# A streaming encoder step: token halves carried through the whole second layer, with S5, gated unit, norms and outputs of one half placed in the feed-forward passes of the other

## The chip, the cores and the metric

The kernel runs as one program on 1 core of a Trainium2 chip. The metric is the device time of one execution in microseconds. Five engines run their own instruction streams and meet at semaphores: PE (matrix products), DVE (vector work), ACT (activations, casts and some DMA issues), POOL (further vector work and some DMA issues) and SP (which issues most DMAs).

## What is computed

1088 tokens (1024 of a prompt, 64 of a running stream) of width 1024 go through two layers. Cut to what matters here:

```python
def swiglu(h, w_gate, w_up, w_down):            # w_gate, w_up: 1024 x 2816
    return (jax.nn.silu(h @ w_gate) * (h @ w_up)) @ w_down

def s5_mixer(h, ...):                           # 64 groups of 16 channels, 64 complex states each
    x = einsum('gpc,blgc->blgp', bb, ug)        # complex, into the states
    s = associative_scan(s_t = a * s_(t-1) + x_t)
    y = real part of einsum('gcp,blgp->blgc', c, s) + d_skip * u
    gl = gelu(y) @ w_glu                        # 1024 x 2048
    ga, gb = split(gl, 2)
    return ga * sigmoid(gb), s_last

# layer 0: x += attention heads and spatial gating, joined by one output projection; x += swiglu(rmsnorm(x))
# layer 1: x += s5_mixer(rmsnorm(x)); x += swiglu(rmsnorm(x))
# y = rmsnorm(x); also the new keys, values, gating rows and the last S5 states
```

## The kernel before

Activations lie transposed: 1024 features are 8 tiles of 128 partitions, tokens run along the free axis. A dense product is made of three single-pass products (`three`, L251 to L253): high part of the weights by high part of the input, the same by the low part, low part of the weights by the high part. Weights come in slabs of 512 KB: SP loads one (L234, two buffers `raw`), ACT makes the high part `whi` (L241), POOL subtracts and leaves `wlo` (L245); SP may load slab t only when POOL has made `wlo` of slab t - 2, and a slab's buffers come free when PE has left the slab four (in layer 1 six) before. A slot of the middle stage is the work on one slab, or on half of one.

The stages in time: input projection; a middle stage whose order a planner writes as a list of slots; S5; GLU; norm 3; feed-forward of layer 1; output.

The middle stage (`SLOTS`, `mid_sp`, `mid_act`, `mid_pool`, `mid_dve`, `mid_pe`) holds attention, output projections and layer 0's feed-forward. It works on two token halves: A has 512 tokens, B 576 in chunks of 288 + 288 (`HCH`). Half A's feed-forward pass runs beside the last attention steps, then comes B's output projection (`outB`, 8 slots of one slab), then half B's pass. A pass has 66 slots: gate, up, gate, up, and two of down, 11 times. Each engine walks the list and does its share of every slot (so does SP: the slab for two slabs on, then what else the slot names). Three banks of PSUM take the results in turn; ACT takes up gates, DVE ups (product) and downs (sum into x). The other half's squares, norm sums and scaled tiles lie in slots of the pass that runs. `mst` (L1211) is the gathered mixer output, and L1315 makes its low part lB for `outB`.

S5 (`s5_sp`, `s5_pe`, `s5_act`, `s5_pool`, `s5_dve`) then takes all 1088 tokens, 8 time steps folded into the partitions, so that 136 columns are left, in 8 units of 8 groups. In each unit PE transposes B (L1829), multiplies C by powers into a kernel K (L1837), makes x (L1849) and y (L1867 with the shift matrix `tm`, L1869 with the states `sh`); K goes through DVE (`kt`) and eight DMAs of SP (L1802) into `tm`; u, C and E come by DMA (L1787, L1776); DVE runs the scan (L1949 to L1983: products L1931, scans L1964 and L1965). y goes out to memory in eight DMAs and comes back reordered. GLU, norm 3 and the feed-forward of layer 1 work on all tokens in chunks of 384/384/320; GLU's inputs hlo are made by L2018, its result is added to x by L2064, and L349 adds squares. The output transposes 9 tiles of 128 (the last 64) tokens (L2081).

## Time and profile before

| | us |
|---|---|
| median of 3 runs | 2808.97 (2808.0 to 2819.7) |
| the profiled execution | 2815.95 |
| its span in the trace | 2814.2 |
| PE matmul busy | 2569.8 (91%) |
| PE weight load busy | 2368.4 (84%) |
| DVE, ACT, POOL busy | 1165.5 (41%), 879.8 (31%), 1108.1 (39%) |
| mean granted clock of PE | 0.938 of full speed |

The slices of the page show where an engine was busy over the span, in tenths; each is 70 us. Busy time of PE counts matmuls whose ends are modelled. A row of the timeline gives start and duration, and in brackets the idle time before with what released it. "Records" of a plain fp32 product are two to an instruction.

### The profile page before, as it was taken

Reading aid. Unit: us, or ns where it says so; the run is one execution under the profiler, and the core shown is the slowest. Engines: PE = TensorE matmul, PEld = TensorE weight load, DVE = VectorE, ACT = ScalarE, POOL = GpSimd, SP = SyncE. Lnnn points to the kernel's source line nnn. Section 1 sums busy time; section 2 is a strip of 40 time slices with the busy share of each in tenths; the row PEclk is TensorE's granted clock in tenths of the full one; section 3 lists DMA queues with packets and bytes.
Section 4 is the critical chain, followed back from the end, with each engine's and each line's share of the span. In section 5 each row is a group of like instructions: output and inputs, shape, how many; then the busy total and the mean of one; then the engine's idle time right before and its main releaser. Section 6 shows DMA issues by size and latency. Waiting matters only on the chain.

```text
span 2814.2 us, 38283 instructions
## 1 busy us (share of the span) xinstructions
PE 2569.8 (91%) x15274; PEld 2368.4 (84%) x15274; DVE 1165.5 (41%) x1877; ACT 879.8 (31%) x1304; POOL 1108.1 (39%) x770
## 2 busy tenths in 40 slices
PE   6998948989997999999999588799699999999998
PEld 4898936667776978999999466799599999999997
DVE  3696636665562142422222677322412222222224
ACT  3422236688893332212211221311311111111114
POOL 2555534554464565544444200333532222222223
PEclk9999969989998999999999676899899999999999
DMA  4315665313423223322222575311111111111111
GB/s 121 103 59 202 240 185 130 86 51 101 104 72 130 85 75 98 107 89 78 86 83 70 162 203 148 125 46 46 30 42 42 44 41 42 44 45 45 45 45 64
DMA packets 290435, 254.10 MB, mean 90 GB/s; under 512 B 32560, under 2 KB 254704, under 8 KB 289024
## 3 DMA queue, kind: packets, MB, share of 16 engines
q1 hardware_dynamic: 264624, 201.73, 24.5%
q0 software_dynamic: 7088, 31.15, 2.9%
q10 hardware_dynamic: 18592, 19.40, 2.9%
q8 instruction: 91, 1.49, 0.2%
q14 instruction: 40, 0.33, 0.0%
HBM read 195.08 MB, written 54.80 MB: 89 GB/s over the span
## 4 chain that ended last, share of the span: by engine, by line
PE 74%; DVE 10%; DMA 5%; POOL 4%; ACT 3%; issue 2%; SPq 1%; ACTq 1%; POOLq 0%; DVEq 0%
PE ps L251 22%; PE ps L253 22%; PE ps L252 22%; PE ps L983 2%; DVE v L1931 1%; PE ps L995 1%; PE ps L1869 1%; DMA mst<-mT 1%; DVE fbuf L423 1%; POOL hlo L431 1%; PE ps L1867 1%; DVE t L1706 1%; POOL ssum L349 1%; DMA dC<-co 1%; PE ps L975 1%
## 5 line engine op out<-in xcount | busy, mean ns | idle before, releaser
L245 POOL TENSOR_TENSOR wlo<-raw,whi 128x1024 fp32r<-128x1024 f32 x250 | 606.1, 2434 | 428.1 <-ACT whi L241 426.4
L251 PE MATMUL ps<-hhi,whi 128*128 128x384 f32 (+1 forms) x1920 | 636.7, 332 | 49.0 <-POOL hlo L2018 14.8
L252 PE MATMUL ps<-hlo,whi 128*128 128x384 f32 (+1 forms) x1920 | 632.3, 329 | 0.0
L253 PE MATMUL ps<-hhi,wlo 128*128 128x384 f32 (+1 forms) x1920 | 632.2, 329 | 0.0
L251 PEld LDWEIGHTS ps<-hhi,whi 128*128 128x128 f32 x1920 | 365.9, 191 | 54.7 <-issue 22.2
L252 PEld LDWEIGHTS ps<-hlo,whi 128*128 128x128 f32 x1920 | 365.9, 191 | 0.3 <-issue 0.2
L253 PEld LDWEIGHTS ps<-hhi,wlo 128*128 128x128 f32 x1920 | 365.6, 190 | 0.0
L241 ACT ACTIVATE whi<-raw 128x1024 fp32r<-128x1024 f32 x250 | 259.1, 1053 | 319.2 <-PE ps L253 141.1
L251 PE MATMUL ps<-hB,whi 128*128 128x288 f32 x832 | 247.4, 297 | 12.2 <-POOL lB L1315 12.2
L509 POOL TENSOR_TENSOR gl<-fbuf,gh 128x384 f32 (+3 forms) x66 | 63.8, 967 | 490.3 <-DVE gh L564 490.3
L253 PE MATMUL ps<-hB,wlo 128*128 128x288 f32 x832 | 246.6, 296 | 0.0
L252 PE MATMUL ps<-lB,whi 128*128 128x288 f32 x832 | 246.5, 296 | 0.0
L561 DVE TENSOR_TENSOR fbuf<-ps,abuf 128x384 f32<-128x384 f32 (+1 forms) x66 | 35.3, 535 | 453.5 <-ACT abuf L479 449.2
L479 ACT ACTIVATE abuf<-ps 128x384 f32<-128x384 f32 (+1 forms) x66 | 31.2, 474 | 561.5 <-PE ps L253 561.5
L251 PE MATMUL ps<-rh,whi 128*128 128x288 f32 (+1 forms) x528 | 177.6, 336 | 15.4 <-DVE xA L1363 6.4
L572 DVE TENSOR_TENSOR x<-ps,x 128x384 f32<-128x384 f32 (+1 forms) x264 | 141.2, 535 | 110.0 <-PE ps L253 108.8
L1353 DVE TENSOR_TENSOR fb<-ps,ab 128x288 f32<-128x288 f32 (+1 forms) x66 | 35.3, 535 | 363.4 <-PE ps L253 339.8
L252 PE MATMUL ps<-rl,whi 128*128 128x288 f32 (+1 forms) x528 | 175.3, 332 | 0.0
L253 PE MATMUL ps<-rh,wlo 128*128 128x288 f32 (+1 forms) x528 | 175.1, 332 | 0.0
L253 PE MATMUL ps<-gh,wlo 128*128 (+2 forms) x528 | 172.2, 326 | 0.0
L251 PE MATMUL ps<-gh,whi 128*128 (+2 forms) x528 | 172.1, 326 | 0.0
L252 PE MATMUL ps<-gl,whi 128*128 (+2 forms) x528 | 172.1, 326 | 0.0
(315 smaller groups left out, 4803.6 us busy)
## 6 DMA issues: line engine op xcount, KB each, us to landing
raw<-in_ffn_w_gate SPq DMA_DIRECT2D x66, 512.0 KB, 3.9
raw<-in_ffn_w_up SPq DMA_DIRECT2D x66, 512.0 KB, 3.9
raw<-in_ffn_w_down SPq DMA_DIRECT2D x66, 512.0 KB, 3.6
raw<-in_ab_w_in SPq DMA_DIRECT2D x20, 512.0 KB, 4.2
raw<-in_ab_w_out SPq DMA_DIRECT2D x16, 512.0 KB, 3.7
raw<-in_ssm_w_glu SPq DMA_DIRECT2D x16, 512.0 KB, 3.9
dC<-co POOLq DMA_DIRECT2D x4, 1152.0 KB, 4.5
ca<-dC SPq DMA_DIRECT2D x8, 576.0 KB, 4.9
```

Of the source, the lines that this page charges most:

```text
L241: act.activation(whi[:, slot(t), :], raw[:, t % 2, :], ACT.Copy).then_inc(sem("w_hi"), 1)
L245: pool.tensor_tensor(wlo[:, slot(t), :], raw[:, t % 2, :], whi[:, slot(t), :].bitcast(F32), ALU.subtract).then_inc(sem("w_lo"), 1)
L251: pe.matmul(out, wh, rh, start=first, stop=False)
L252: pe.matmul(out, wh, rl, start=False, stop=False)
L253: return pe.matmul(out, wl, rh, start=False, stop=last)
L349: pool.tensor_tensor(ssum[:, c, 0:n], ssum[:, c, 0:n], sqbuf(k, a)[:, 0:n], ALU.add).then_inc(sem("n_add"), 1)
L479: act.activation(abuf[:, v % 2, 0:n], ps[:, 2 * (v % 2), 0:n], ACT.Silu).then_inc(sem("pair_act"), 1)
L509: pool.tensor_tensor(gl[:, bass.ds(o, n)], fbuf[:, v % 2, 0:n], gh[:, bass.ds(o, n)].bitcast(F32), ALU.subtract).then_inc(sem("hid_lo"), 1)
L561: dve.tensor_tensor(fbuf[:, v % 2, 0:n], ps[:, 2 * (v % 2) + 1, 0:n], abuf[:, v % 2, 0:n], ALU.mult).then_inc(sem("pair_used"), 1)
L572: dve.tensor_tensor(xo, acc(v)[:, 0:n], xo, ALU.add).then_inc(sem("acc_used"), 1)
L983: mm = pe.matmul(out, mat[:], r, start=mat is tri and u["first"] and j == 0, stop=True, skip_group_check=True)
L1353: dve.tensor_tensor(fb2[:, h % 2, 0:n], out, ab2[:, h % 2, 0:n], ALU.mult).then_inc(sem("use_v"), 1)
```

## The change

The last serial stages are dissolved into the slot list. There are four passes of 66 slots now: layer 0 half A, layer 0 half B, layer 1 half A, layer 1 half B. All work of layer 1 that isn't a pass is put into slots of the pass that runs:

- S5 of half A (64 columns) stands in the pass of layer 0, half B; S5 of half B (72 columns, starting from the scan state that half A leaves) in the pass of layer 1, half A. A unit begins in a gate slot with x (PE, ACT's copy, DVE's scan), y follows two slots later, the next unit's loads three, the return of y four and six slots later; one unit every six slots.
- GLU of half A stands in 16 slots before the last three stages of the pass of layer 0, half B; GLU of half B likewise in the pass of layer 1, half A. Norm 3 of a half has its 8 tiles per chunk in the slots behind: for A four a slot, for B eight a slot.
- Output tiles of half A stand in the pass of layer 1, half B; those of half B at the end.
- The tables of S5 (B transposed, and the shift matrix of K) are made once for both halves, in 8 steps two slots apart in and around the slots of `outB`, and kept in memory (`dBT`, `dT`); both halves load them (`s5_load`).
- Chunks of half B are 256 + 320. All 332 slabs use four buffers. Activation tables are preloaded by ACT only in steps after another table was used. The tokens x stay in SBUF between the layers.

The diff cut to its core:

```diff
 HALF = [(0, 512), (512, 576)]
-HCH = [[(0, 512)], [(512, 288), (800, 288)]]
+HCH = [[(0, 512)], [(512, 256), (768, 320)]]
...
+        passes = [(0, 0), (0, 1), (1, 0), (1, 1)]
+
+        def sequence():
+            for no, (layer, half) in enumerate(passes):
+                if no != 1:
+                    yield "pair", layer, half, 0
+                for i in range(PARTS):
+                    yield "pair", layer, half, 2 * i + 1
+                    if i + 1 < PARTS:
+                        yield "pair", layer, half, 2 * i + 2
+                    elif no == 0:
+                        yield ("pair", *passes[1], 0)
+                    yield "down", layer, half, i
...
+                soon(5, pl=[0])
+                for f in range(KD):
+                    soon(7 + 2 * f, pre=[f])
+                    if f + 1 < KD:
+                        soon(8 + 2 * f, pl=[f + 1])
+                    soon(8 + 2 * f, psh=[f])
+                    soon(9 + 2 * f, pst=[f])
...
+            for k, h, at in list(stage["rms"]):
+                if now >= at:
+                    stage["rms"].remove((k, h, at))
+                    rms_slot(k, h)
+                    end = norm_soon(k, h, 1, 8 if (k, h) == (3, 1) else 4)
+                    if k == 2:
+                        soon(end, hs=[h])
+                        soon(end + 1, sl=[8 * h])
+                        stage["f"][h], stage["free"][h] = 0, len(SLOTS) + end + 3
+
+        def run_glu(h):
+            stage["glu"][h] = -1
+            glu(h)
+            rms_slot(3, h)
+            norm_soon(3, h, 1, 4 * (h + 1))
...
+                for h in range(2):
+                    f = stage["f"][h]
+                    if gate and f is not None and f < KD and len(SLOTS) >= stage["free"][h]:
+                        F = 8 * h + f
+                        work["sx"] = [F]
+                        stage["f"][h], stage["free"][h] = f + 1, len(SLOTS) + 5
...
+                for F in work.get("sx", []):
+                    soon(2, sy=[F])
+                    if F % KD < KD - 1:
+                        soon(3, sl=[F + 1])
+                    soon(4, sz=[F])
+                    soon(6, sg=[F])
+                    if F % KD == KD - 1:
+                        for i in range(4):
+                            soon(7 + i, ys=[KD * (F // KD) + 2 * i, KD * (F // KD) + 2 * i + 1])
+                        stage["glu"][F // KD] = len(SLOTS) + 8
...
+                for f in S["psh"]:
+                    pre_shift(sp, f)
+                for f in S["pst"]:
+                    pre_store(sp, f)
+                for f in S["pl"]:
+                    pre_load(sp, f)
+                for h in S["hs"]:
+                    h_store(sp, h)
+                for F in S["sl"]:
+                    s5_load(sp, F)
...
+        def pre_load(sp, f):
+            if f == 0:
+                sp.wait_ge(sem("u_pv"), NU)
+                sp.wait_ge(sem("ms_lo"), 12)
+            else:
+                sp.wait_ge(sem("s_K"), f)
+            js = slice(4 * f, 4 * f + 4)
+            sp.dma_start(br[:], dB[:, js, :, :]).then_inc(sem("br_in"), 16)
+            sp.dma_start(cp[:], dC[:, js, :, :]).then_inc(sem("cp_in"), 16)
...
+        def pre_pe(pe, f):
+
+            pe.wait_ge(sem("br_in"), 16 * (f + 1))
+            if f:
+                pe.wait_ge(sem("e_BT"), 2 * f)
+                pe.wait_ge(sem("e_K"), 2 * f)
+            else:
+                pe.wait_ge(sem("u_c"), NU)
+                pe.wait_ge(sem("u_t"), NU)
+            for q in range(8):
+                mm = pe.transpose(ps[:, 3 + q // 4, (q % 4) * P:(q % 4 + 1) * P], br[:, q // 2, q % 2, :], ident[:])
+            mm.then_inc(sem("s_B"), 1)
+            pe.wait_ge(sem("cp_in"), 16 * (f + 1))
+            for g in range(8):
+                j, a = divmod(g, 2)
+                r = slice(64 * a, 64 * a + 64)
+                for q in range(2):
+                    mm = pe.matmul(ps[0:16, 5 + a, j * P:(j + 1) * P], br[r, j, q, P - 16:P], cp[r, j, q, 0:P],
+                                   start=q == 0, stop=q == 1)
+            mm.then_inc(sem("s_K"), 1)
...
+        def pre_shift(sp, f):
+
+            sp.wait_ge(sem("e_BT"), 2 * f + 2)
+            sp.dma_start(dBT[:, 4 * f:4 * f + 4, :, :], btp[:]).then_inc(sem("bt_out"), 16)
+            sp.wait_ge(sem("e_K"), 2 * f + 2)
+            if f:
+                sp.wait_ge(sem("t_out"), 16 * f)
+            else:
+                sp.wait_ge(sem("t_zero"), 1)
+            for s in range(L):
+                sp.dma_start(tmp[16 * s:16 * s + 16, :, 16 * s:P], kt[0:16, :, 0:P - 16 * s]).then_inc(sem("t_made"), 16)
...
+        def s5_x_pe(pe, F):
+            h, f = divmod(F, KD)
+            nn = NN[h]
+            pe.wait_ge(sem("bt_in"), 16 * (F + 1))
+            pe.wait_ge(sem(f"u_in{F % 2}"), 16 * L * (F // 2 + 1))
+            if F:
+                pe.wait_ge(sem("e_X"), banks_of(F - 1))
+            else:
+                pe.wait_ge(sem("e_BT"), 2 * KD)
+            for q in range(2):
+                for j in range(4):
+                    o = (4 * q + j) * nn if h == 0 else j * nn
+                    for a in range(2):
+                        mm = pe.matmul(ps[64 * a:64 * a + 64, 3 + (q if h else 0), o:o + nn],
+                                       bt[h][:, j, q, 64 * a:64 * a + 64], u[h][:, F % 2, 2 * j + a, :], start=True, stop=True,
+                                       skip_group_check=True)
+            mm.then_inc(sem("s_X"), 1)
...
+        def s5_y_pe(pe, F):
+            h, f = divmod(F, KD)
+            nn = NN[h]
+            pe.wait_ge(sem("tm_in"), 16 * (F + 1))
+            pe.wait_ge(sem("ca_in"), 16 * (F + 1))
+            pe.wait_ge(sem("s_sh"), F + 1)
+            if F:
+                pe.wait_ge(sem("e_Y"), 2 * F)
+            else:
+                pe.wait_ge(sem("e_K"), 2 * KD)
+            for g in range(8):
+                j, a = divmod(g, 2)
+                r = slice(64 * a, 64 * a + 64)
+                out = ps[:, 5 + a, j * nn:(j + 1) * nn]
+                pe.matmul(out, tm[h][:, g, :], u[h][:, F % 2, g, :], start=True, stop=False)
+                for q in range(2):
+                    mm = pe.matmul(out, ca[h][r, j, q, :], sh[h][r, q, j, :], start=False, stop=q == 1)
+            mm.then_inc(sem("s_Y"), 1)```

In `s5_scan` DVE does, per unit: a copy and a memset for the decay, four products and two sums of 256 (half A) or 288 (half B) elements, two scans, four products and two sums, and the copies into `sh` (half B also a few of 4 elements for the sample's start and the carried state). `s5_y_act` issues the eight DMAs of y on ACT.

How the order changes. First SP, before, around `outB`: mixer outputs and the slabs of `w_out` (L234) alone, then the slabs of the feed-forward.

```order
L1211 DMA mst<-mT 128x576 x2
L234 DMA raw<-in_ab_w_out 128x8x128
L1211 DMA mst<-mT 128x576 x2
L234 DMA raw<-in_ab_w_out 128x8x128 x4
L234 DMA raw<-in_ffn_w_gate 128x8x128
L234 DMA raw<-in_ffn_w_up 128x8x128
```

SP in the same place now (dBT is the store of the transposed B, tmp<-kt the shifted copies of K, br and cp the loads for the next step, dT the store of the shift matrix):

```order
L1476 DMA dBT<-btp 128x1024
L1483 DMA tmp<-kt 16x1024
L1483 DMA tmp<-kt 16x8x112
L1483 DMA tmp<-kt 16x8x96
L1483 DMA tmp<-kt 16x8x80
L1483 DMA tmp<-kt 16x8x64
L1483 DMA tmp<-kt 16x8x48
L1483 DMA tmp<-kt 16x8x32
L1483 DMA tmp<-kt 16x8x16
L1429 DMA br<-dB 128x1024
L1430 DMA cp<-dC 128x1152
L234 DMA raw<-in_ab_w_out 128x8x128
```

Ten further DMAs stand between two slabs, and every second slab has them (the other has the store of dT ahead of it); the loads of br and cp are the last of them.

PE, before, where S5 begins (behind the last sums of layer 0): all table steps, x and y in a row.

```order
L1829 MATMUL ps<-ident,br 128x128 x8
L1837 MATMUL ps<-ca,br 16x128 x16
L1849 MATMUL ps<-u,bt 64x136 x16
L1867 MATMUL ps<-u,tm 128x136
L1869 MATMUL ps<-sh,ca 128x136 x2
```

PE now, first a table step in a slot of `outB`, between products of 320 and of 256 columns:

```order
L252 MATMUL ps<-lB,whi 128x320
L253 MATMUL ps<-hB,wlo 128x320
L1442 MATMUL ps<-ident,br 128x128 x8
L1449 MATMUL ps<-cp,br 16x128 x16
L251 MATMUL ps<-hB,whi 128x256
```

and the x step of S5's first unit in a gate slot of layer 0, half B (its y step, L1562 and L1564, stands two slots on):

```order
L252 MATMUL ps<-lB,whi 128x320
L253 MATMUL ps<-hB,wlo 128x320
L1543 MATMUL ps<-u,bt 64x64 x16
L251 MATMUL ps<-hB,whi 128x256
L252 MATMUL ps<-lB,whi 128x256
```

The table step needs br of that step, and what PE does next stands behind it; the x and y steps stand ahead of the products of their slots in the same way.

## Rows read from the trace of the kernel before

**Rows 1.** The page: busy shares, granted clock by slice, the chain that ended last

```profile
PE 2569.8 (91%) x15274; PEld 2368.4 (84%) x15274; DVE 1165.5 (41%) x1877; ACT 879.8 (31%) x1304; POOL 1108.1 (39%) x770
...
PEclk9999969989998999999999676899899999999999
...
PE 74%; DVE 10%; DMA 5%; POOL 4%; ACT 3%; issue 2%; SPq 1%; ACTq 1%; POOLq 0%; DVEq 0%
```

**Rows 2.** Busy time by stretch: from:to length, PE PEld DVE ACT POOL, PEclk, DMA, GB/s

```profile
1168.00:1555.00 387.00, 383.81 (x2873) 383.11 (x2872) 115.45 (x255) 77.69 (x105) 178.53 (x105) 0.99 0.26 78
1555.40:1780.40 225.00, 158.80 (x999) 120.35 (x998) 153.56 (x282) 46.60 (x98) 17.98 (x21) 0.70 0.63 168
1969.00:2020.00 51.00, 27.59 (x130) 23.15 (x129) 28.25 (x30) 20.98 (x38) 28.97 (x30) 0.82 0.00 0
2785.00:2814.20 29.20, 16.71 (x113) 14.90 (x111) 9.29 (x16) 12.91 (x24) 5.53 (x7) 0.82 0.40 153
```

**Rows 3.** PE: dense stretches at all chunks, 512, 288 columns (window rows); starts in the timeline

```profile
2030.00:2770.00 740.00, 740.00 (x4496) 1.00 0.14 43
1060.00:1100.00 40.00, 40.00 (x178) 1.00 0.32 95
1480.00:1520.00 40.00, 40.00 (x304) 1.00 0.27 80
...
1780.42 0.66 PE L251 MATMUL ps<-hhi,whi 128*128 128x384 f32 x1 [14.84 <-POOL hlo L2018]
...
688.66 0.28 PE L983 MATMUL ps<-sphi,comp 128*128 128x256 f32 x1
688.78 0.28 PE L983 MATMUL ps<-splo,comp 128*128 128x256 f32 x1
...
664.64 0.28 PE L983 MATMUL ps<-splo,comp 128*128 128x64 f32 x1
664.75 0.28 PE L983 MATMUL ps<-sphi,comp 128*128 128x64 f32 x1
```

**Rows 4.** PE by stretch: transposes and K; the y step; the x step

```profile
1646.00:1650.80 4.80, 4.42 (x40) 0.64 1.14 276
1635.00:1643.60 8.60, 8.60 (x48) 1.00 0.68 137
1652.28:1654.40 2.12, 2.08 (x32) 1.00 1.07 326
```

**Rows 5.** Timeline of POOL and SP's queue, and from the page a DMA's landing

```profile
945.49 2.41 POOL L245 TENSOR_TENSOR wlo<-raw,whi 128x1024 fp32r<-128x1024 f32 x1
...
947.92 0.37 SPq L234 DMA_DIRECT2D raw<-in_ffn_w_gate  x1
...
1692.02 5.65 SPq L1802 DMA_DIRECT2D tm<-kt  x8
...
br<-dB SPq DMA_DIRECT2D x8, 512.0 KB, 4.1
```

**Rows 6.** Timeline of DVE in a unit's scan: products, scan

```profile
1637.42 1.48 DVE L1931 TENSOR_TENSOR v<-xx,e 128x544 f32<-128x544 f32 x2
...
1641.98 1.29 DVE L1964 TENSOR_TENSOR_SCAN w<-r,v 128x544 f32<-128x544 f32 x1
...
1650.76 0.17 DVE L1983 COPY sh<-p 128x4 f32<-128x4 f32 x1
```

**Rows 7.** Timeline of DVE and POOL: one sum of DVE without and with POOL

```profile
1801.31 0.56 DVE L2064 TENSOR_TENSOR x<-x,fbuf 128x384 f32<-128x384 f32 x1
...
1863.96 1.01 POOL L349 TENSOR_TENSOR ssum<-ssum,sq 128x384 f32<-128x384 f32 x1 [2.62 <-ACT sq L339]
...
1864.10 1.29 DVE L2064 TENSOR_TENSOR x<-x,fbuf 128x384 f32<-128x384 f32 x1
```

**Rows 8.** Timeline of POOL: half B's norm tiles of layer 0, first and last

```profile
985.03 1.56 POOL L1341 TENSOR_TENSOR lB<-nf,hB 128x288 fp32r<-128x288 f32 x2 [1.60 <-ACT hB L1305]
...
1009.90 1.58 POOL L1341 TENSOR_TENSOR lB<-nf,hB 128x288 fp32r<-128x288 f32 x2 [0.87 <-ACT hB L1305]
```

## What I expect of the change, and why

> **What bounds the kernel now.** I read the page's busy shares and slices first [rows 1]: PE is busy 2569.8 of 2814.2 us, and the chain of work that ended last is 74% PE. PEclk, near full from slice 17 on, falls to 6, 7 and 6 in slices 22 to 24. The table by stretch says what they are [rows 2]. From 1168 to 1555 us (feed-forward of layer 0, two token halves in turn) PE lacks 3.2 us of 387. Then S5 stands alone: from the end of that stage (1555.4) to GLU's first product (1780.42, which waited 14.84 us for its low half, [rows 3]) 225.0 us pass with PE busy for 158.8 at clock 0.70 and DVE for 153.6. Norm 3 between GLU and the last feed-forward costs some 23 of 51 us; from 2030 to 2770 PE is dense [rows 3]; the outputs take 29.2 us with PE busy for 16.7. So what can be won lies in S5's stretch, the norm behind GLU and the tail. Elsewhere PE is full, and whatever is put in there is added to the end.
>
> **Base.** The sum is made against the span of 2814.2 us; the profiled run took 2815.95 us, and the median of the runs shown is 2808.97, 7 us less.
>
> **1. Removed: -259.** The serial S5 stretch goes, 225.0. GLU and the last feed-forward stay in work: 1152 + 4752 products, which in the dense stretch take 740 us per 4496, 0.1646 each [rows 3], so 972 us. From 1780.4 to 2786 pass 1005.6; the 33.6 of idle time in it, at norm 3 and at starts, go too. 2814.2 - 258.6 = 2555.6.
>
> **2. Added S5 work on PE: +171.** This is now inside full passes, so all of it counts. Before, one unit's y step of all tokens (24 instructions, 48 records) takes 8.60 us at 136 columns and full clock; the x step (32 records) 2.08 [rows 4]. Now each of 8 units runs twice, at 64 and at 72 columns: the instructions double and the columns of each halve. How much does half the columns save? If a record were bound by its columns, all that is left is 64/136. But with the 128x128 weight load in front, products of 256 columns start 0.12 apart and such of 64 still 0.11 [rows 3]: there is a floor of about 0.11 per record, 5.3 for the y step. From above it is 8.6, unchanged; taking 72 columns at 0.44 ns (0.226 at 512, [rows 3]) off each of 48 records gives 7.1 and at 72 columns left 7.2 to 7.3, which I take, since 0.179 per record at 136 columns is far over what 136 columns need and so is load more than columns. x: 1.9, between 1.0 and 2.1. 16 x 9.1 = 146. The tables once: 8 steps of transposes and K, 4.42 at clock 0.64 [rows 4], so between 2.8 and 4.4 at full clock; I take 3.1, 25.
>
> **3. The table steps stall PE in the out-projection of half B: +65.** Steps f = 0..7 stand two slots apart (a slot is one slab, 24 products of 256 and 24 of 320 columns; half B's 288 take 0.132, half A's 512 0.226 [rows 3], so 320 take 0.146, and with 0.117 for 256 that makes 6.3 us of PE). The load of br for step f+1 stands on SP in the slot between, behind three things: that slot's slab, whose issue waits for POOL's wlo two slabs back; the store of the transposed B; and eight kt to tmp copies. In the trace a slab leaves SP right behind POOL's wlo (945.49 + 2.41, then SP at 947.92, [rows 5]); I place that 4.3 into the slot, since ACT's high part (1.05) and wlo can begin only when PE has left the slab four back. Then 0.4 + 0.5 + 5.1 (eight kt copies took 5.65 in one row; I take a little less, since there they ran beside seven other loads), 0.5 for br, 4.1 landing: br lands 14.9 after that slot's start. PE is there after 6.3, so it waits 8.6. Steps 2 to 6 pay 8 to 10, step 0 some 4 (behind the loads of the mixer's output), 1 and 7 little: 50. Each such stop is followed by a stretch at 1.2 GHz, as in the K step here, 0.64; 2 per stop, 15. If nothing were queued before br this would be 0; if clock recovery is slow, 90.
>
> **4. The scan stalls PE in half B's units: +51.** A unit is x in a gate slot, y two slots later. y needs the DVE scan. The rows of one scan at 544 elements [rows 6] give 0.16 + 1.04 ns per element for a product (0.73), 1.29 for a scan; from the first product (1637.42) to the end of the last copy (1650.93) pass 13.5, with the copies ahead some 14.6. With 256 elements (half A) it is 8.8, with 288 (half B, four more small ones) 10.6. x ends at 1.9, ACT's copy at 2.9. Half A's units run in half B's slots: y stands at 2 x 6.3 + 1.9 = 14.5, scan done at 11.7 plus what delays it; about even, +4 for eight. Half B's run in half A's slots of 24 x 0.226 = 5.4: y stands at 12.7, the scan is done at 13.5 at best. And it isn't at best: the same sum of two operands takes DVE 0.56 us with POOL idle and 1.29 when POOL's add of 1.01 began 0.14 before it [rows 7]. POOL has a wlo of 2.4 [rows 5] and often a low half (1.01 at 384 elements, so 1.3 at 512) in each slot, so I add 4.1: 17.6 against 12.7, 4.9 x 8 = 39, and 8 for the clock. The Trainium skill (SBUF — State Buffer, "Who interferes with whom") says that a DVE instruction with two SBUF inputs and a GpSimd one that reads SBUF exclude one another for a whole instruction; the pair of rows agrees (0.73 longer). By the rule the stall is 4.9, without it 0.8 per unit.
>
> **5. Edges: +33.** The norm between GLU and feed-forward was a stop of 23 us once. Now both halves have one, and each is given slots of the other half as cover. Half B's 16 tiles of 288 take POOL from 985.03 to 1009.90 + 1.6, 26.4 us with slabs between [rows 8]. They are given two slots of 5.4: 15.5 short. Half A has 8 tiles in two slots of 6.3, little short: +6. The sums of squares stand right behind GLU's last product, which DVE, ACT and POOL must still take up: 4 each, 8. The split of y before GLU, 4.
>
> **6. Output, tables of ACT: -19.** Four of nine output tiles go into the last pass: +6 on PE there, -8 of the 29.2. Chunks: 0.226 + 0.117 + 0.146 = 0.489 for 3 x 0.1646 over 1968 triples of layer 1, and next to nothing in layer 0: -9. Fewer table loads of ACT in the attention steps, where PE lacks little: -8, between 0 and 20.
>
> The sum is 2555.6 + 171 + 65 + 51 + 33 - 19 = 2857 of span; 2858 as a run, less 7 for the median: about **2850**. 259 us of serial and idle time are exchanged for 171 of PE work in full passes and 149 of new waits.
>
> **Rivals.** (a) The waits are covered. If SP's slab issue stands earlier in its slot than I place it, and the scan fits its two slots, terms 3 and 4 shrink to some 10: 2850 - 105 = 2745, faster. For it: in the full stretch DVE works 115 us of 387 and POOL 179 [rows 2]. Against: the queue order of SP, ten DMAs in a slot of 6.3 us. Chance 0.25, with what lies between 2745 and 2795.
> (b) Small products scale with their columns. At 512 columns a product takes 0.226, 0.44 ns per column; 64 to 72 columns would be 0.03, and (48 + 32) x 0.03 x 16 = 38 instead of 146: 2742, faster. The Trainium skill (TensorE: Matmul & The Clock Gate, "Wait — 56ns, not 53.3ns?") gives N over 2.4 GHz plus 2.5 ns for start to start. The rows at 64 columns (0.11) speak against: 0.07.
> (c) The other side, slower than my sum. A unit's y step delays PE's slot, ACT issues eight DMAs behind it (0.6 to 0.7 each as SP's, 5.65 for eight, [rows 5]) before it takes the next whi, and whi sets wlo and so SP. If ACT's whi comes 3 us late in each of 16 units, with the half clock behind each stop: +60, 2910. It decides where y ends under 5 us before the slot does. 0.15.
> (d) The change doesn't move the time much: half of 3 and 4, between 2795 and 2823: 0.13.
> The forecast with its own range (2823 to 2885) has 0.40.
>
> **How the numbers follow.** What this kernel's measurement can tell from no change is about 0.5%, 14 us: below 2795 is faster, 2795 to 2823 the same. (a) + (b) = 0.32 faster; (d) = 0.13 same; forecast and (c) = 0.55 slower. The range leaves out half of (b) and the ends of (a) and (c): 2735 to 2915.
>
> **What would show each step.** 1: no stretch of several slices with PE under 7 between 1550 and 1800; PE's share over 93%. 2: y steps of 7.2 and x of 1.9 at full clock, some 145 in all; under 60 is (b). 3: L1442 (transposes) with idle time released by the DMA of br, 8 us a time. 4: the first y product waiting for DVE: about 5 a unit in half A's slots, near 0 in half B's. 5: waits for POOL's low halves ahead of layer 1's pass B. 6: the tail under 22. (c) shows as waits of L251 for wlo after y steps. The prediction is wrong if the waits of 3 and 4 together are under 60, if y is near 5, or if a wait stands where I have none: behind ACT, for the loads of u and tables, or at GLU's slabs.

## The result, and the profile after

The changed kernel takes 2959.36 us (median of 4 runs, 2956.4 to 2961.9) against 2812.63 of the kernel before: ratio 1.0511, 95% interval 1.0491 to 1.0532. It is slower, as forecast, but by 147 us and not by 41: 2959 lies above the range, which ended at 2915. Its profiled span is 2958.3 us.

The page of the changed kernel, busy shares and granted clock by slice (one digit is 74 us):

```profile
PE 2683.7 (91%) x15914; PEld 2397.4 (81%) x15914; DVE 1233.3 (42%) x2098; ACT 900.7 (30%) x1327; POOL 1310.1 (44%) x848
...
PE   6997958899996679999999998999999898999998
...
PEclk7998969899998789999898999978878899999999
```

PE's hollow in the serial stretch is gone, and yet its share of the span is 91%, as before, and it has 114 us more of busy time than in [rows 1], for 640 more records. The clock row tells where to look: behind the table steps (slices 12 to 14) it has digits 7 and 8 in eight more slices from 19 to 31, and PE has a 9 in seven of them. The table by stretch (from:to length, PE busy, granted clock, DMA, GB/s), first all table steps, then half A's units (first to last y), half B's, and last the tail (its first 8 us are still dense products):

```profile
913.80:1090.00 176.20, 118.47 (x831) 0.82 0.45 138
...
1297.00:1683.00 386.00, 386.00 (x2708) 0.89 0.39 110
1932.00:2326.00 394.00, 369.88 (x1665) 0.83 0.39 109
...
2930.00:2958.30 28.30, 16.75 (x106) 0.81 0.23 85
```

In the second row PE isn't idle for one moment in 386 us, and still runs a fifth of it at half speed. Against [rows 2], where the serial stretch had 0.70 with PE idle for 66 of 225 us, this is a loss of another kind. What PE waited for (total us, times, longest):

```profile
PE ps L1442 <- DMA br<-dB: 73.4, 7, 16.1
PE ps L1562 <- DVE own_mark L1681: 27.8, 8, 3.8
```

These are the table steps (forecast: 50) and the y steps of half B, which wait for the scan (forecast: 39). SP's queue ahead of a table step, answering to [rows 5]:

```profile
1010.80 0.33 SPq L234 DMA_DIRECT2D raw<-in_ffn_w_down  x1
1011.18 0.43 SPq L1476 DMA_DIRECT2D dBT<-btp  x1
1011.71 5.64 SPq L1483 DMA_DIRECT2D tmp<-kt  x8
1017.39 0.59 SPq L1429 DMA_DIRECT2D br<-dB  x1
```

Here br leaves 6.2 us behind the slab, as the prediction laid it out. And a y step of half A, in the timeline of PE, whose rows answer to [rows 4]:

```profile
1300.80 0.43 PE L1562 MATMUL ps<-u,tm 128*128 128x64 f32 x2
1301.16 0.66 PE L1564 MATMUL ps<-sh,ca 64*128 64x64 f32 x4
1301.75 0.43 PE L1562 MATMUL ps<-u,tm 128*128 128x64 f32 x2
...
1302.83 0.69 PE L1562 MATMUL ps<-u,tm 128*128 128x64 f32 x2
1303.45 1.11 PE L1564 MATMUL ps<-sh,ca 64*128 64x64 f32 x4
1304.49 0.69 PE L1562 MATMUL ps<-u,tm 128*128 128x64 f32 x2
...
1306.53 0.41 PE L252 MATMUL ps<-rl,whi 128*128 128x256 f32 x1
1306.74 0.41 PE L253 MATMUL ps<-rh,wlo 128*128 128x256 f32 x1
```

A group of six records takes 0.95 us at first (1300.80 to 1301.75) and 1.66 further on (1302.83 to 1304.49). With no wait before or in the step, the granted clock, 1.00 of full speed at its start, is 0.50 from the middle of it on, which is the lower level, 1.2 GHz. The dense products behind it start out at that speed: the last two rows begin 0.21 us apart, where products of 256 columns at full clock begin 0.12 apart.

### The profile page after: what moved, and what is told of

Its sections match the earlier page's. It is cut to its first block, busy times and chain, and to the rows that moved or that the text cites. A ratio compares the mean times of both kernels' runs of the same rounds, so it can differ in the third digit from the quotient of the medians.

```text
span 2958.3 us, 39375 instructions
## 1 busy us (share of the span) xinstructions
PE 2683.7 (91%) x15914; PEld 2397.4 (81%) x15914; DVE 1233.3 (42%) x2098; ACT 900.7 (30%) x1327; POOL 1310.1 (44%) x848
## 2 busy tenths in 40 slices
PE   6997958899996679999999998999999898999998
## 4 chain that ended last, share of the span: by engine, by line
PE 73%; DVE 10%; DMA 5%; POOL 5%; ACT 2%; SPq 2%; issue 2%; ACTq 0%; POOLq 0%; DVEq 0%
PE ps L251 20%; PE ps L252 19%; PE ps L253 19%; PE ps L1564 4%; PE ps L746 2%; PE ps L1562 2%; POOL wlo L245 2%; PE ps L758 1%; SPq L1483 1%; DMA mst<-mT 1%; DMA br<-dB 1%; DVE vw L1653 1%; DVE nf L1324 1%; PE ps L738 1%; PE ps L1449 1%
## 5 line engine op out<-in xcount | busy, mean ns | idle before, releaser
L245 POOL TENSOR_TENSOR wlo<-raw,whi 128x1024 fp32r<-128x1024 f32 x332 | 800.6, 2413 | 858.9 <-ACT whi L241 857.5
L251 PE MATMUL ps<-hB,whi 128*128 128x320 f32 (+1 forms) x1792 | 535.3, 299 | 6.5 <-POOL lB L1722 6.5
L252 PE MATMUL ps<-lB,whi 128*128 128x320 f32 (+1 forms) x1792 | 532.2, 297 | 0.0
L253 PE MATMUL ps<-hB,wlo 128*128 128x320 f32 (+1 forms) x1792 | 532.2, 297 | 0.0
L241 ACT ACTIVATE whi<-raw 128x1024 fp32r<-128x1024 f32 x332 | 346.9, 1053 | 524.2 <-PE ps L253 372.2
L251 PE MATMUL ps<-rh,whi 128*128 128x512 f32 (+2 forms) x1056 | 370.1, 350 | 32.9 <-POOL rl L1227 12.5
L252 PE MATMUL ps<-rl,whi 128*128 128x512 f32 (+2 forms) x1056 | 362.6, 343 | 0.0
L253 PE MATMUL ps<-rh,wlo 128*128 128x512 f32 (+2 forms) x1056 | 361.4, 342 | 0.0
L251 PE MATMUL ps<-hA,whi 128*128 128x512 f32 x896 | 356.4, 398 | 1.6 <-POOL lA L1722 1.6
L252 PE MATMUL ps<-lA,whi 128*128 128x512 f32 x896 | 349.8, 390 | 0.0
L251 PEld LDWEIGHTS ps<-hB,whi 128*128 128x128 f32 x1792 | 341.9, 191 | 9.5 <-POOL lB L1722 7.5
L253 PE MATMUL ps<-hA,wlo 128*128 128x512 f32 x896 | 349.3, 390 | 0.0
L252 PEld LDWEIGHTS ps<-lB,whi 128*128 128x128 f32 x1792 | 342.0, 191 | 0.7 <-issue 0.5
L253 PEld LDWEIGHTS ps<-hB,wlo 128*128 128x128 f32 x1792 | 341.8, 191 | 0.0
L251 PEld LDWEIGHTS ps<-rh,whi 128*128 128x128 f32 x1056 | 215.1, 204 | 57.2 <-issue 22.9
L252 PEld LDWEIGHTS ps<-rl,whi 128*128 128x128 f32 x1056 | 215.6, 204 | 14.4
L253 PEld LDWEIGHTS ps<-rh,wlo 128*128 128x128 f32 x1056 | 214.1, 203 | 16.2
## 6 DMA issues: line engine op xcount, KB each, us to landing
raw<-in_ffn_w_gate SPq DMA_DIRECT2D x88, 512.0 KB, 3.8
raw<-in_ffn_w_up SPq DMA_DIRECT2D x88, 512.0 KB, 3.8
raw<-in_ffn_w_down SPq DMA_DIRECT2D x88, 512.0 KB, 3.3
raw<-in_ssm_w_glu SPq DMA_DIRECT2D x32, 512.0 KB, 4.0
raw<-in_ab_w_in SPq DMA_DIRECT2D x20, 512.0 KB, 4.2
raw<-in_ab_w_out SPq DMA_DIRECT2D x16, 512.0 KB, 4.0
bt<-dBT SPq DMA_DIRECT2D x16, 512.0 KB, 5.0
tm<-dT SPq DMA_DIRECT2D x16, 512.0 KB, 4.2
```

What stands on the lines that cost most here:

```text
L241: act.activation(whi[:, slot(t), :], raw[:, t % 2, :], ACT.Copy).then_inc(sem("w_hi"), 1)
L245: pool.tensor_tensor(wlo[:, slot(t), :], raw[:, t % 2, :], whi[:, slot(t), :].bitcast(F32), ALU.subtract).then_inc(sem("w_lo"), 1)
L251: pe.matmul(out, wh, rh, start=first, stop=False)
L252: pe.matmul(out, wh, rl, start=False, stop=False)
L253: return pe.matmul(out, wl, rh, start=False, stop=last)
```

## The experiments

All ratios are to the kernel before, measured beside it. "After" is the changed kernel, 2959.

**The loads of the table steps.**

```diff
             for S in SLOTS:
+                for f in S["pl"]:
+                    if f:
+                        pre_load(sp, f)
                 for t in S["slabs"]:
...
                 for f in S["pl"]:
-                    pre_load(sp, f)
+                    if f == 0:
+                        pre_load(sp, f)
```

> One edit of order on SP: the loads of br and cp for table step f+1 (f from 0 on) are issued at the head of the slot between, ahead of its slab, the store of the transposed B and the eight kt to tmp copies, and no longer behind them. Theory: the ten DMAs ahead of them are what makes PE wait 73.4 us for br in seven of eight table steps, and each wait takes PE's clock to half for some 10 us more (eight stretches, 92 us in that region, up to 35 us lost on dense products). Without the queue the load is issued some 5 us into the slot of the step itself and lands before the next step's slot: the wait falls to under 10 us, the half clock with it; 2959 - 65 - 30 = about 2860. Rival: it is the landing of the load and PE's own release of br that bound it, not the queue; then the wait only halves and the time is about 2915.

Measured: 2892.0 us, ratio 1.0262 (1.0240 to 1.0284), 67 less. The wait fell from 73.4 to 20.8 us:

```profile
PE ps L1446 <- DMA br<-dB: 20.8, 2, 16.1
```

16.1 of it is step 0, whose load can't start earlier: it waits for the mixer's outputs. The gain is 53 of waits and 14 besides. The 14 are the clock's: from the end of attention to the last table step (851 to 1090 us after the change, 851 to 1023 here) PE's busy time falls from 159 to 146 us for the same work, and its granted clock rises from 0.83 to 0.93. The queue was the cause.

**Where y stands: spread out, or a slot later.** In e2 the eight groups of y are put between the gate products of the slot; e4 moves the step, and with it the next unit's loads and the return of y, one slot later.

```diff
+                def between():
+                    turn[0] += 1
+                    if parts and turn[0] % len(gs) == 0:
+                        parts.pop(0)()
...
-                    dense_pe(pe, g)
+                    dense_pe(pe, g, between=between if parts else None)
```

> One edit of order on PE: the y step of a unit no longer stands in a row ahead of its slot's products; its eight groups of three instructions are put one behind each eighth of the gate products of the same slot. ACT takes y up behind the gates of the slot. The same instructions run. Theory: the y step, 7.6 us of small products, itself takes the clock to half (in the changed kernel the clock falls some 5 us into a y step with no wait before it, and stays down for 10 us in half A's units and 17 in half B's, 92 + 133 us in all), and dense products pay for it. Mixed with dense products it should not: the half clock goes (about -95) and half B's first y product stands later than the scan (27.8 us of waits go): about 2840. Rival: y costs only its own work, and the clock falls by waits: then only the waits and what follows them go, about 2900 to 2930.

> Both edits: the loads of the table steps at the head of their slot on SP, and the groups of y spread over the gate products on PE. If the two causes are separate places they add: e1's gain plus e2's, about 2740 by the first theories, and so under the kernel before (2812). If the rivals hold in both, 2860 to 2890.

```diff
-                    soon(2, sy=[F])
+                    soon(3, sy=[F])
                     if F % KD < KD - 1:
-                        soon(3, sl=[F + 1])
+                        soon(4, sl=[F + 1])
-                    soon(4, sz=[F])
+                    soon(5, sz=[F])
-                    soon(6, sg=[F])
+                    soon(7, sg=[F])
...
```

> y one slot later (three behind x), still in a row; the next unit's loads, y's return and what follows one slot later too. It takes away PE's wait for the scan (27.8 us in half B's units) and leaves everything else. Theory (y itself takes the clock down): the wait goes, the half clock behind half B's y steps shrinks to that of half A's (17 to 10 us each), half A's stay: about -28 - 20, 2910. Rival (the wait takes the clock down): half B's half clock goes altogether, 133 us of it: -28 - 55, 2875. A third: loads of the next unit, issued a slot later, become a new wait of the x step: above 2940.

Measured: e2 2925.0 (1.0387, 1.0357 to 1.0416), e3 2864.5 (1.0153), e4 2944.6 (1.0443, 1.0421 to 1.0464). Spreading gained 35, not 120: half A's clock, first row here, is 0.91 where it was 0.89, so it falls with y among dense products, too; half B's rose to 0.90 and its wait fell only to 19.4:

```profile
1298.00:1680.00 382.00, 382.00 (x2725) 0.91 0.39 111
1922.00:2291.00 369.00, 348.94 (x1671) 0.90 0.41 117
```

e3, with this edit and that of e1, shows that the two nearly add (67 + 35 against 95). In e4 the wait for the scan is gone, yet 15 us is all that it gave. The x step now sat idle for 24.7, which the profile puts down to issue; it is the wait for its loads, since one unit's eight DMAs of u are issued from 1961.50 to 1966.69, take 4.7 to land, and x starts at 1971.5. Down products also waited 10 us more for DVE's sums. So it was the third expectation of e4, above 2940, that came. Half A's stretch in e4 has a clock of 0.91 with hardly a wait in it (379.5 of 381 us busy), which speaks for y itself.

**Is it y?** e5 leaves out two of three products of half A's y step; e6 widens the columns under the same loads.

```diff
-                pe.matmul(out, tm[h][:, g, :], u[h][:, F % 2, g, :], start=True, stop=False)
-                for q in range(2):
+                mm = pe.matmul(out, tm[h][:, g, :], u[h][:, F % 2, g, :], start=True, stop=h == 0)
+                for q in range(2 * h):
```

> The changed kernel with two thirds of half A's y step left out (the two products of ca and sh of each group, 16 of 24 instructions; the states' part of y is missing for half A), nothing else. Theory: a y step costs its own work and, by taking the clock to half for some 10 us behind it, about 4 more; with 2.5 us of small products left the clock should hold, so 8 x (5.1 + 4) = 73 less than 2959: about 2886, and the half-clock stretches of half A's pass (8 of 7 to 14 us) gone. Rival: the half clock there has another cause (the x step, or DMA traffic of the unit's loads): only the work goes, 41: about 2918, and the stretches stay.

Measured: 2879.0 us, ratio 1.0239 (1.0220 to 1.0258), 80 less. What is left of the step takes 1.7 us in place of 7.6, so the work alone would give 8 x 5.9 = 47 (not the 41 expected). The step, and the stretch of half A's units:

```profile
1300.90 1.89 PE L1562 MATMUL ps<-u,tm 128*128 128x64 f32 x16
1302.60 0.36 PE L251 MATMUL ps<-rh,whi 128*128 128x256 f32 x1
...
1301.00:1607.00 306.00, 306.00 (x2477) 1.00 0.49 138
```

The clock is full throughout. The loads, the x steps, the DMAs of each unit are all still there, so it is y's products that take the clock down, and here they cost 1.7 times what they take themselves.

```diff
-                out = ps[:, 5 + a, j * nn:(j + 1) * nn]
+                w = 2 if j < 3 else 1
+                out = ps[:, 5 + a, j * nn:(j + w) * nn]
```

> On top of the earlier loads of the table steps (2892): in the y step the products of the first six of eight groups run over twice the columns (128 and 144 in place of 64 and 72; the surplus columns fall on the next group's place, which that group then writes anew). The same number of instructions and weight loads, more columns under each load. If the clock falls because a y step drives few columns per weight load, half A's half-clock stretches (about 86 us) and half B's (about 125) shorten or go; each us of them is worth half a us, and the columns themselves cost little, 0.03 per record, 36 records, 1 us per y step (+17): by this theory 2892 + 17 - 70 = about 2840. Rival: the clock falls by the kind or number of small products (fp32, alternating 128 and 64 rows), whatever their columns: 2892 + 17 = about 2910, stretches as before.

Measured: 2883.2 us (1.0252, 1.0228 to 1.0276), 9 less than e1 (by the ratios 3), not 50. By halves the effect is there. First half A, then half B:

```profile
1232.00:1597.00 365.00, 365.00 (x2721) 0.97 0.42 116
...
1843.00:2252.00 409.00, 384.94 (x1662) 0.82 0.38 105
```

In half A the clock is 0.97 with more columns under the same loads, and 386 us shrink to 365 although there is more work. In half B, where PE first waits for the scan (28.1 us in eight units), it is 0.82 (0.84 in e1), and the stretch is 17 us longer than e1's 392. So both seem to be at work: y's own products, and in half B the wait ahead of them.

**y behind its slot's products.**

```diff
-                for F in S["sy"]:
-                    s5_y_pe(pe, F)
                 for n, g in enumerate(gs):
...
+                for F in S["sy"]:
+                    s5_y_pe(pe, F)
                 for h in S["os"]:
```

> e6 and the y step behind the gate products of its slot in place of ahead of them, so 5.4 us later in half B's units. PE's wait for the scan there (27.4 us in eight units) goes; what follows each wait (3 to 7 us of half clock more in half B's units than in half A's) goes with it: e6 less 35 to 50. Rival: y's results come 5.4 us later, the next unit's loads too, and x waits for u as it does when y stands a whole slot later (24.7 us there): e6 within 15.

> e7 and the eight table steps two slots later. What is left of the wait for br, 20.8 us, is nearly all of step 0 (16.1), whose load can start only when the mixer outputs are in; two slots (12.6 us) later it should be there: e7 less 12 to 25 (the clock falls once less, too). Rival: outB's own products wait for the mixer's low halves at that place, as before the change (7.9 us in one wait); then PE waits there instead: e7 within 8.

(ACT takes y up behind the gates of that slot, too.) Measured: e7 2864.2 (1.0185), e8 2862.3 (1.0180): 19 and 2. Half B's stretch in e7 bears out the wait's part in the clock, 0.94 where e6 had 0.82. But the wait for the scan went, and another took its place, in both:

```profile
1860.00:2240.00 380.00, 337.51 (x1676) 0.94 0.41 115
...
PE ps L251 <- DVE fb L1261: 41.0, 10, 6.4
```

Units begin in the second gate slot of a group; behind it come an up slot and then down. The expectations of e10, e13 and e15 say that the down products need that up product. They don't need its data: the unit begins at the gate of pair 2i + 2, while in `dense_pe` the down products behind it wait only for pair 2i + 1, and in the trace of e7 the first two of them start without a wait.

```profile
1852.43 0.39 PE L251 MATMUL ps<-rh,whi 128*128 128x512 f32 x1
...
1857.09 0.50 PE L251 MATMUL ps<-rh,whi 128*128 128x512 f32 x1 [1.78 <-DVE fb L1261]
...
1856.27 0.06 DVE L1688 MEMSET own_mark<- 128x1 f32 x1
1856.35 0.69 DVE L1261 TENSOR_TENSOR fb<-ps,ab 128x512 f32<-128x512 f32 x1
```

It is the third down product that stops. With three banks of PSUM it needs the bank that the up product lies in, and DVE takes that product up (fb) only behind the whole scan, whose last instruction is own_mark. In the changed kernel this didn't show, since PE waited for the scan itself at that place. e8, which has in addition

```diff
-                    soon(7 + 2 * f, pre=[f])
+                    soon(9 + 2 * f, pre=[f])
```

and so for pl, psh and pst, brought the wait for br from 21.5 to 9.1 but gained only 2 us; 5.7 of it came back as waits of L251 for wlo and at issue (counted from 850 us on), the rest I can't place.

**The order inside y.**

```diff
-            for g in range(8):
-                j, a = divmod(g, 2)
-                r = slice(64 * a, 64 * a + 64)
-                out = ps[:, 5 + a, j * nn:(j + 1) * nn]
-                pe.matmul(out, tm[h][:, g, :], u[h][:, F % 2, g, :], start=True, stop=False)
-                for q in range(2):
-                    mm = pe.matmul(out, ca[h][r, j, q, :], sh[h][r, q, j, :], start=False, stop=q == 1)
+            for j in range(4):
...
+                outs = [ps[:, 5 + a, j * nn:(j + w) * nn] for a in range(2)]
+                for a in range(2):
+                    g = 2 * j + a
+                    pe.matmul(outs[a], tm[h][:, g, :], u[h][:, F % 2, g:g + w, :].rearrange("p g n -> p (g n)"), start=True, stop=False,
+                              skip_group_check=True)
+                for q in range(2):
+                    for a in range(2):
+                        r = slice(64 * a, 64 * a + 64)
+                        mm = pe.matmul(outs[a], ca[h][r, j, q, :], sh[h][r, q, j:j + w, :].rearrange("p j n -> p (j n)"), start=False,
+                                       stop=q == 1, skip_group_check=True)
```

> The changed kernel with another order inside the y step alone: the six products of two groups are issued as tm, tm, then C re of the one group (rows 0 to 63) beside that of the other (rows 64 to 127), then both C im, in place of three of the one group and three of the other. Same 24 instructions, same columns. The x step, whose neighbours alternate between two halves of the array, takes 0.06 us per record; the y step, whose two C products stand on the same 64 rows, takes 0.158. Theory: the step is bound by loads and products that can't overlap on the same rows; alternating, the 32 C records fall to about 0.08 and the step from 7.6 to 5.0 us: 16 x 2.6 = 42, and less half clock: 2959 - 50 = about 2910. Rival: a 128-column load is the floor (0.11 to 0.16) whatever the rows: within 10 of 2959.

Here w is 1. Measured: 2860.2 us, ratio 1.0155 (1.0132 to 1.0178): 99 less, twice the forecast, from a new order of 24 instructions. A row pair of the timeline and the stretches of half A and half B:

```profile
1299.76 0.66 PE L1568 MATMUL ps<-sh,ca 64*128 64x64 f32 x8
1300.35 0.66 PE L1563 MATMUL ps<-u,tm 128*128 128x64 f32 x4
...
1299.00:1628.00 329.00, 329.00 (x2729) 1.00 0.46 129
...
1876.00:2232.00 356.00, 331.90 (x1665) 0.86 0.43 121
```

Eight C records now take 0.59 us (0.074 each), where four took 0.59 (1301.16 to 1301.75) before; four tm records take 0.59, too (0.148 each, 0.18 before). Two groups take 1.18 in place of 1.90, the step 4.7 in place of 7.6. Half A keeps the full clock, 386 us become 329: 8 x 2.9 = 23 of y's work, so 34 of clock. In half B the wait and the clock behind it stay (0.86).

**Cutting the scan.** The second part of the scan goes behind the next slot's up product. In e10, which is e8 with this, y and the next unit's loads stand a slot later, too; e11 is e10 with the order of e9.

```diff
-                    soon(2, sy=[F])
+                    soon(1, s2=[F])
+                    soon(3, sy=[F])
...
+                for F in S["s2"]:
+                    s5_scan(dve, F, 1)
                 for F in S["sg"]:
```

> e8 (2862) with DVE's scan in two parts: the first (products) in x's slot, the second (scans and rotation back) one slot later and behind that slot's up product; y stands behind the products of the third slot behind x. In e8 PE waits 40.1 us for DVE's up product (fb), which stands behind the whole scan, while the down products need it. Theory: with the scan cut there, those waits go, and the half clock behind them (eight stretches of 7): 2862 - 40 - 20 = about 2800. Rival: the scan is simply late by the port shared with POOL, and the second part delays y and the next unit: waits move to y or x, 2850 or more.

> e10 with the order of e9 inside the y step. If both hold they add: e10 less 40, about 2760, below the kernel before by 2%. If the order of e9 does nothing, e10 within 10.

> e12 with y behind the products of its slot in place of ahead (no wait for the scan) and DVE's scan cut in two, the second part behind the next slot's up product (so that the down products don't wait for it). Theory: the 27.5 us wait for the scan in half B's units and the 10 to 14 us of half clock behind each go: e12 - 27 - 30 = about 2730. Rival: the up product of the slot is at hand only at its end, so the second part of the scan starts late and PE waits for it at y all the same: e12 within 15.

e13 is e12 (below) with y behind its slot's products, still two slots behind x, and the scan cut. Measured: e10 3062.0 (1.0872), e11 3000.0 (1.0665), e13 2892.7 (1.0271). All are far slower: e10 and e11 by 200 and 138 us than e8, e13 by 97 than e12. My theory fell. The waits of e13:

```profile
PE ps L251 <- DVE xA L1274: 60.1, 11, 7.5
PE ps L251 <- DVE xB L1274: 56.0, 10, 6.2
```

The second part can begin only when the up product is at hand, at the end of its slot, and then the sums of the down products (xA, xB) stand behind it: with three banks PE stops at the fourth down product. In e10 x also sat idle for 67.2 us. As in e4, its loads now stand a slot later in SP's list: the eight of u are issued from 2003.08 to 2008.32, ten us after y of the unit before was through (1993.31), and x starts at 2011.75.

**Do the gains add, and was the order of y a loss before, too?**

> The two edits that gained most, together: the loads of the table steps ahead on SP, with the eight steps two slots later (wait for br from 73 to 9 us), and the y step with its C products alternating between the two halves of the rows (4.7 in place of 7.6 us, and no half clock behind it in half A's units). If both act at places of their own: 2959 - 68 - 5 - 99 = about 2787, 1% below the kernel before. If part of the clock's loss is shared, 2800 to 2830: then the change is still no gain.

> The kernel before with the same new order inside its y step (C products of two groups alternating between the halves of the rows), nothing else. There the y step takes 8.6 us of PE in each of eight units, but the stretch is bound by the chain of scan (14.6 us), loads and shifted copies, with PE busy for 159 of 225 us: if y stands beside the next scan, nothing moves (ratio 1.00, within 0.3%); if it is on the chain of each unit, 8 x 3 = 24 us less, ratio 0.991.

e12 has the loads of e1, the order of e9 and also e8's table steps two slots later, for which its sum counts 5. Measured: e12 2795.8 us, ratio 0.9921 (0.9897 to 0.9944): 164 less than after, of 172 by the sum, and 0.8% faster than the kernel before. e14 2801.1, ratio 0.9943 (0.9924 to 0.9962): 14 to 16 us of gain for the same order in the kernel before, between its two expectations, so part of y stood on the chain there. With that order on both sides, e12 gains nothing that is clear of noise.

**The first gate slot.** e15 is e12 with y behind its slot's products and

```diff
-                    if gate and f is not None and f < KD and len(SLOTS) >= stage["free"][h]:
+                    if gate and n % 2 and f is not None and f < KD and len(SLOTS) >= stage["free"][h]:
```

> e12 (2796) with each unit begun in the first gate slot of a group of six (gate, up, gate, up, down, down) in place of the second, and y behind the products of the second gate slot. Then four slots lie between x and the first down products, which need the up products that stand behind the scan on DVE, and y is asked for 5.4 us later than now. e7 and e13 showed that a later y alone moves the wait to what stands behind the scan on DVE. Theory: the 27.8 us of waits for the scan go without taking their place elsewhere, and with them most of the half clock in half B's units (some 100 us, 40 lost); the last unit ends later, so the norms behind GLU have two slots less of cover, +15 to +25: 2796 - 28 - 40 + 20 = about 2750. Rival: DVE is late for the up products at any place, because scan and port conflict fill it: 2790 or more.

Measured: 2803.7 us, ratio 0.9960 (0.9942 to 0.9977). The waits for DVE at the units are gone, and it is still no faster than e12. From 850 us on PE waits for wlo:

```profile
PE ps L251 <- POOL wlo L245: 39.2, 17, 5.0
```

In e12 it was 9.3 from there on. (Waits around the norms and GLU, which have less cover now, come to 50 where e12 had 34.) That is the prediction's rival (c): ACT waits for y, issues eight DMAs and only then makes the next whi. From the timeline of ACT in a unit of half B:

```profile
1868.15 0.72 ACT L1592 ACTIVATE yy<-ps 128x288 f32<-128x288 f32 x2 [3.99 <-PE ps L1572]
1868.90 3.75 ACTq L1596 DMA_DIRECT2D dY<-yy  x8
1872.75 2.00 ACT L241 ACTIVATE whi<-raw 128x1024 fp32r<-128x1024 f32 x2 [3.88 <-issue]
```

ACT was idle for 4.0, busy with y for 4.5, and wlo began at 1873.88.

```diff
                     soon(2, sy=[F])
+                    soon(3, y2=[F])
...
+                for F in S["y2"]:
+                    s5_y_act(act, F)
                 for F in S["sz"]:
...
-                for F in S["sy"]:
-                    s5_y_act(act, F)
```

> e15 (2804) with one edit on ACT: taking up y and issuing its eight DMAs stands in the slot behind y, after that slot's high part of the weights, in place of the end of y's slot. In e15 ACT waits 4.0 us for the end of y, spends 0.7 + 3.75 on it and only then makes the next high part; POOL's wlo follows it and PE waits for wlo 39.2 us in 17 places, 2.7 at most units of half B. That is rival (c) of the prediction, now with its place. Theory: those waits go to under 12: about 2804 - 30 = 2774. Rival: y's return is then late for DVE (which reads it two slots on) and its wait stands in front of the up products: 2795 or more.

Measured: 2755.9 us, ratio 0.9797 (0.9780 to 0.9814): 48 less than e15, 2% under the kernel before. The waits for wlo from 850 us on fell to 9.6, and the stretches of half A and half B are:

```profile
1264.00:1594.00 330.00, 330.00 (x2729) 0.99 0.45 129
1849.00:2138.00 289.00, 289.00 (x1671) 1.00 0.51 150
```

Half B's units, the row with 394 us at clock 0.83 in the changed kernel, take 289 at 1.00 without a wait. That is the change as it was meant: it pays when y and scan cost neither waits nor clock. Part of the 2% isn't the change's own, though: the order of y gains 0.6% in the kernel before, too (e14), and against that e16 is 1.5% faster (0.9797 to 0.9943).

## Why the prediction was right in direction and wrong in size

The sum was 2857 of span; it came to 2958. Term by term:

**1, removed work: held.** No hollow is left where the serial stretch was. Its other sign, PE's share over 93%, didn't come: it is 91%, with 144 us of waits under 3 to 5 below.

**2, PE's work: held.** y was forecast at 7.2 and takes 7.6 at full clock (eight groups of 0.95), x 1.9 and takes 1.1 (1283.13 to the next row at 1284.21): 16 x 8.7 = 140 for 146. A table step takes 1.97 + 3.18 at half clock, so some 2.6 at full, for 3.1. Rival (b) is out: y isn't near its columns. But the reason given, load more than columns, wasn't all of it: e9 shows 32 of the 48 records at half their time with the same loads and columns, once neighbours stand on different halves of the rows.

**3, table steps: mechanism right, size short.** 73.4 of waits for 50, in the first step 16.1 (forecast 4) and about 9.5 in six others (8.6). The clock behind them, forecast at 15, agrees with the 14 that e1 gained beside its waits. +23 over the forecast.

**4, the scan: the wait right, its clock wrong.** 27.8 where 39 (half B) and 4 (half A) were forecast: about 3.5 a unit in half B, none in half A. The port's share is in the trace, in a unit of half B (DVE, and POOL beside it):

```profile
1972.97 2.22 DVE L1642 TENSOR_TENSOR xx<-xx,p 128x4 f32<-128x4 f32 x1
1975.22 0.17 DVE L1642 TENSOR_TENSOR xx<-xx,p 128x4 f32<-128x4 f32 x1
...
1978.16 0.76 DVE L1652 TENSOR_TENSOR_SCAN vw<-r,xx 128x288 f32<-128x288 f32 x1
1978.83 2.89 DVE L1653 TENSOR_TENSOR_SCAN vw<-r,xx 128x288 f32<-128x288 f32 x1
...
1972.71 2.46 POOL L245 TENSOR_TENSOR wlo<-raw,whi 128x1024 fp32r<-128x1024 f32 x1
...
1978.63 2.48 POOL L245 TENSOR_TENSOR wlo<-raw,whi 128x1024 fp32r<-128x1024 f32 x1 [3.46 <-ACT whi L241]
```

The same addition of 4 elements takes 0.17 and 2.22, the same scan 0.76 and 2.89. The long addition ends with POOL's wlo (1975.19 and 1975.17), the long scan 0.61 behind it (1981.72 and 1981.11), about its own time. That is 2.05 + 2.13 = 4.2 us in the unit, for the 4.1 forecast from [rows 7]. This is what the Trainium skill (SBUF — State Buffer, "Who interferes with whom") states, an exclusion for the whole instruction, and the trace agrees.

The failed step stands in the same term: "and 8 for the clock", worth about 100. The prediction let the clock fall only where PE stops, and gave nothing to half A's y steps. By the two rows of the stretches, 0.89 over 386 us is 85 us at half speed, all of them busy, so 42 lost; 0.83 over 394 is 134, less what PE was idle, so 55 to 67. About 100 where 8 stood. With +23 for the table steps and -11 for the shorter scan waits this makes 2857 + 92 + 23 - 11 = 2961 for 2958.3. That it closes to 3 us is partly luck: half B's clock is known only to 12 us, and the smaller differences are left out (-6 and -4 of work, -4 for half A's scans, +10 of edges, some +8 of the last term). e5 and e9 confirm the larger share from the other side: y's products alone, cut or sped up, give back by the clock 33 us beside 47 of work (e5) and 53 beside 46 (e9). None of the signs that the prediction named for being wrong would have shown this loss: all of them are waits or lengths of steps, and half A's y steps wait for nothing. The table [rows 4] held the hint: 0.179 us per record was too long for a load that other rows had at 0.11, and the question what PE did in the rest wasn't asked.

**5, edges: held.** Waits for the low halves, squares and sums around norms and GLU come to 43 (12.5, 8.1 and 9.0 by POOL, 13.8 by DVE) for 33 forecast; of DVE's part 9.5 stood in the kernel before.

**6: held in part.** Attention ends 8.6 us earlier (its last product starts at 852.3 for 860.9), for 8 forecast; that the table loads did it is not shown. The tail, from the end of the last dense product, takes 20.5 us (2937.81 to 2958.3) where it took 26.0 (2788.18 to 2814.2): 5.5 less, for 8. Products of 256 columns start 0.12 apart, as [rows 3] shows, and not 0.117, so the chunks can save only about 4 of the 9.

**Rivals.** (a), that the waits are covered, didn't hold for the kernel as built; only e16, with all the edits above, gets near its 2745. (c) didn't show in the changed kernel: from 850 us on PE waited 6.6 us for wlo, and it seems that PE's own wait for the scan covered ACT's delay. In e15, where that wait is gone, it cost 30 us of waits (39.2 for 9.3), and e16 gained 48 by removing it.

## What to carry to other kernels

When small products are moved from a stretch in which PE idles into full passes, their price is their time and what they do to PE's clock for the dense products behind them; read the granted clock of the stretch, not only its busy share, since PE was 100% busy here at 0.89. Look at the order among such products first: neighbours that use different halves of the rows took half the time of neighbours on the same half. On an engine that takes its instructions in order a wait that is removed shows the next one behind it (scan, up product, down sums, ACT's DMAs). So ask before each move which instruction stands behind the moved one, and whether PE needs its data or only the bank that it frees.

## What was unexpected of the hardware

- A stretch of 386 us in which PE never idles ran at a mean granted clock of 0.89; with a third of y's products 1.00, with the same products faster 1.00, with twice the columns under the same loads 0.97.
- fp32 products over 64 rows into 128 columns took 0.148 us a record in a row on the same rows (four in 0.59) and 0.074 when they alternated between rows 0 to 63 and 64 to 127 (eight in 0.59).
- A DVE addition of 4 elements took 2.22 us beside a POOL subtraction of 2.46, and 0.17 without it.
